# The last 128 tokens of an expert layer take the gathered path instead of the last 96, and are selected first

## The chip, the cores and the metric

The kernel runs on 1 core of one Trainium2 chip. The metric is the device time of the whole program in microseconds, lower is better.

## The reference

Two transformer layers over 512 tokens of width 1024, in float32. The first layer, the two attention mixers of the second and the norms are not touched by the change. The part that matters is the last step, `peer_ffn`: 16384 experts, each one row of `expert_u` and one of `expert_v`; every token has 8 heads, and every head picks 16 experts as sums of two sub-keys.

```python
def peer_ffn(x, w_q, sub_keys, expert_u, expert_v):
    q = _rms((xt @ w_q).reshape(T, P_HEADS, P_KEY_DIM))
    s1 = einsum('thd,hnd->thn', q[..., :half], sub_keys[:, 0])     # T x 8 x 128
    s2 = einsum('thd,hnd->thn', q[..., half:], sub_keys[:, 1])
    v1, i1 = top_k(s1, 16)
    v2, i2 = top_k(s2, 16)
    cand = (v1[..., :, None] + v2[..., None, :]).reshape(T, 8, 256)
    vals, ci = top_k(cand, 16)
    e = take(i1, ci // 16) * 128 + take(i2, ci % 16)               # T x 8 x 16
    g = softmax(vals)
    a = einsum('cd,ckd->ck', xc, expert_u[ec])
    w = gc * gelu(a)
    return einsum('ck,ckd->cd', w, expert_v[ec])
```

## The kernel before

**Layout.** The program runs both layers one after the other; the expert part takes the second half. Engines meet at counted semaphores, and each engine's program is written out by hand in the order in which it runs (`block.tensor` for PE, `block.scalar` for ACT, `block.vector` for DVE, `block.gpsimd` for POOL, `block.sync` for SP, which issues the loads and stores). The tokens lie on the columns of the moving operand, the features on the partitions, except in the selection, where a tile of 128 tokens lies on the partitions.

**Two paths for the experts.** For the first `TD` = 416 tokens (`T` - `RARE`) the kernel computes all 16384 experts: 128 *units* of 128 experts each. A unit of `u_in` is loaded into a ring of four slots (`u_load`), split into a high and a low part (`high` on ACT, line 1393; the low part on POOL in `column`, line 2162, for the first `U_PLAIN` = 52 units, and on DVE in `weight_low`, line 1978, for the others), and multiplied by the high and low parts of the normalised tokens (`u_unit`, 24 matmuls of 416 columns, line 1036). ACT takes the gelu (`gelu_unit`, line 1426), and SP stores it to `gelu` in HBM. The low parts alternate between two buffers, so the split of unit e waits for unit e - 2. The picked gates are put into a table of all experts by products of one-hot matrices: DVE makes those of 16 tokens (`one_hots`, lines 2007 to 2011), PE multiplies them (`spread`, line 1057, two banks of 4 tokens for each unit), ACT evacuates (line 1433), and SP stores a slab of 32 tokens, 2 MB, in two halves of a pair of blocks (`store`). There are `SLABS` = 13 slabs, done beside 4 units each. In the last stage (V) the table and the gelu are loaded again in quads of four units (`quad`), multiplied (`weigh`), split (`w_high`, `low`) and used as the moving operand against units of `v_in` (`v_unit`), 24 matmuls a unit again.

For the last `RARE` = 96 tokens the kernel gathers the picked rows instead. They lie on partitions in two blocks: 64 tokens, each on two partitions, and 32 tokens, each on four (`RARE_BLOCKS`), so that the 128 picks need 64 + 32 = 96 gathers of 128 rows of 4 KB (`rare_slot`). `u_gather` (POOL, line 2173) fetches into one of six slots, `dot` (DVE, line 1986) multiplies by the transposed token and sums; after the gelu and the gates, `v_gather` (line 2183) fetches the rows of `v` and `add_row` (DVE, line 2058) adds them up. At the end PE folds the partitions of a token together with small matmuls (lines 1075, 1076).

**Order.** PE: scores of the keys for four tiles of tokens (line 1011), transposes of the last 96 tokens (lines 1022 and 1028, evacuated by ACT to SBUF), 52 units without one-hots, transposes of the picks (line 1087), 52 units with two banks of one-hot products behind each, 24 units alone, then the 128 units of V. DVE: the selection of tiles 0 to 3 (lines 1906 to 1945) during the first 52 units, then the gates, one-hots, conversions and dots: 6 dots in 8 units in the loop, and the 58 left over spread over the last 23 units. Selection of a tile: the top 16 of 16 lists of 128 (`top16`), all 256 sums, the top 16 of 8 lists of 256, then for both index halves a comparison, a product and a sum over 2048 elements. ACT's Exp of all scores stands behind the gelu of unit 47.

Of the kernel before, what the change touches and what calls it, by code (L numbers as in the profile page):

```python
# [7 lines left out]
ALU = mybir.AluOpType  # L8
# [7 lines left out]
P = 128  # L16
# [34 lines left out]
RARE_BLOCKS = [(64, 2), (32, 4)]  # L51
RARE = sum(n for n, _ in RARE_BLOCKS)
TD = T - RARE
SLABS = TD // TB
RARE_AT = [0, PICKS // 2]
RARE_SLOTS = sum(PICKS // k for _, k in RARE_BLOCKS)
U_SLOTS, V_SLOTS = 6, 6
SPREAD_DOTS = 6
BANK_T = T // N_KEYS
U_PLAIN = 52  # L60
# [81 lines left out]
def rare_slot(s, i=0, per=0):  # L142

    m, r = divmod(s, 3)
    if r < 2:
        return 0, i * (per // 3 * 2) + (RARE_AT[0] + 2 * m + r)
    return 1, i * (per // 3) + (RARE_AT[1] + m)


# [13 lines left out]
def _ready(out):  # L163
# [10 lines left out]
    return "out_ready", base[kind] + j + 1  # L174

# [22 lines left out]
def build(nc, xT_in, par_in, pT_in, cst_in, stream, pos_in, u_in, v_in, rows_in, out, dense, gelu):  # L198
    with ExitStack() as ctx:
# [3 lines left out]
        def sem(name):  # L203
# [116 lines left out]
        cand = sb("cand", [P, E_H, E_K, E_K], c=ch)  # L320
        tv = sb("tv", [P, 2, E_H, E_K], c=ch)
        ti = sb("ti", [P, 2, E_H, E_K], mybir.dt.uint32, c=ch)
        tif = sb("tif", [P, 2, E_H, E_K], BF16, c=ch)
        cv = sb("cv", [P, E_H, E_K], c=ch)
        ci = sb("ci", [P, E_H, E_K], mybir.dt.uint32, c=ch)
        cm = sb("cm", [P, 2, E_H, E_K], mybir.dt.uint32, c=ch)
        cmf = sb("cmf", [P, 2, E_H, E_K], BF16, c=ch)
# [4 lines left out]
        oh = sb("oh", [P, E_H, E_K, E_K], BF16, c=ch)  # L332
        places = sb("places", [P, E_K], BF16, c=ch)
# [10 lines left out]
        wsp = sb("wsp", [P, 2, 2, T], F32R, c=ex)  # L344
        acc = sb("acc", [P, D], c=ex)
        rare = sb("rare", [P, U_SLOTS, D], c=ex)
        ex.close()
        rows_of = [rare[:, k, :] for k in range(U_SLOTS)]
        xts = [hnt[:, :, :].rearrange("p a t -> p (a t)"), xt2[:, :]]
        accs = [acc, acc2]  # L350
        dots, share, place = (rstd[:, k * RARE_SLOTS:(k + 1) * RARE_SLOTS] for k in range(3))
        place = place.bitcast(mybir.dt.uint32)
        folds = [rstd[:, 3 * RARE_SLOTS:3 * RARE_SLOTS + 64], rstd[:, 3 * RARE_SLOTS + 64:3 * RARE_SLOTS + 96]]
# [10 lines left out]
        tk_sub, tk_exp, sel_ready, selt_done = (sem(v) for v in ("tk_sub", "tk_exp", "sel_ready", "selt_done"))  # L364
# [68 lines left out]
        def _(sp_):  # L433
# [118 lines left out]
        def _(pe):  # L552
# [452 lines left out]
            for t in range(TT):  # L1005
# [55 lines left out]
            def v_unit(i, j, first=False, last=False):  # L1061
# [1300 lines left out]
```

## Time and profile before

| | |
|---|---|
| Three runs | 2704.39, 2709.26 and 2712.55 us, median 2709.26 us |
| The profiled execution | 2706.09 us, its span 2704.2 us |
| PE busy | 2585.8 us, 96% of the span |
| PE weight loads busy | 2228.3 us, 82% |
| DVE busy | 1788.3 us, 66% |
| ACT busy | 897.9 us, 33% |
| POOL busy | 1263.4 us, 47% |
| DMA | 491.88 MB, mean 182 GB/s |
| Mean granted clock of PE | 0.985 of full speed |

"Busy" is the time in which an engine runs at least one instruction; matmuls overlap one another in the records, so their mean duration is longer than the distance from one to the next. PEld is the loading of weights, which runs beside the matmuls. The DMA share is the mean busy share of the 16 DMA engines. Times in rows are microseconds from the start of the span.

### The profile page before, as it was taken

The numbers are of one execution on the slowest core, as the hardware profiler recorded it, in microseconds if no ns is written. First come the engines' busy times: TensorE is split into PE (matmuls) and PEld (weight loads), VectorE is DVE, ScalarE is ACT, GpSimd is POOL, SyncE is SP. The second block draws the span as 40 slices with busy tenths as digits, with TensorE's granted clock in tenths as the row PEclk, the third lists the DMA queues.
The fourth block names the chain that finished last, engine by engine and source line by source line (L and its number), as shares of the span: only waits on it lengthen the run. The fifth ranks groups of instructions, "written<-read, shape, count | busy, mean of one in ns | idle before, by whom it ended". The sixth has DMA issues, their size and how long they took to land.

```text
span 2704.2 us, 37346 instructions
## 1 busy us (share of the span) xinstructions
PE 2585.8 (96%) x13264; PEld 2228.3 (82%) x13264; DVE 1788.3 (66%) x2768; ACT 897.9 (33%) x1525; POOL 1263.4 (47%) x615
## 2 busy tenths in 40 slices
PE   6999999999998999998999999999999899999999
PEld 4777778888876777443878999999999899999999
DVE  7899983272234544766448996777778666676766
ACT  2323222101122224665224444344433233333332
POOL 5888888887875541000773555311147222222221
PEclk9999999999999998999999999999999999999999
DMA  4343334333322223000333555899999977887884
GB/s 146 130 138 128 134 122 140 128 107 125 122 100 91 86 86 129 1 1 1 120 116 102 158 159 153 266 301 302 301 343 418 364 296 293 309 303 294 297 300 165
DMA packets 176227, 491.88 MB, mean 182 GB/s; under 512 B 13840, under 2 KB 83600, under 8 KB 176144
## 3 DMA queue, kind: packets, MB, share of 16 engines
q1 hardware_dynamic: 148496, 390.15, 41.6%
q0 software_dynamic: 27648, 100.68, 10.4%
q8 instruction: 46, 0.75, 0.1%
q14 instruction: 37, 0.30, 0.0%
HBM read 434.14 MB, written 56.62 MB: 181 GB/s over the span
## 4 chain that ended last, share of the span: by engine, by line
PE 76%; DVE 7%; issue 7%; POOL 5%; DMA 3%; ACT 2%; SPq 0%; POOLq 0%; DVEq 0%; ACTq 0%
PE ps L1036 31%; PE ps L567 31%; POOL spl L2162 3%; PE ps L965 2%; PE ps L1057 2%; DMA rare<-rows_in,rstd 2%; PE ps L942 1%; PE ps L658 1%; POOL rare L2173 1%; PE ps L925 1%; PE ps L583 1%; DVE hnt L1521 1%; DVE hl L1525 1%; PE ps L921 1%; PE ps L830 1%
## 5 line engine op out<-in xcount | busy, mean ns | idle before, releaser
L567 PE MATMUL ps<-hh,spl 128*128 128x512 f32 x2064 | 654.4, 396 | 19.0 <-DVE hl L1525 7.2
L2095 POOL TENSOR_TENSOR spl<-ring,zero 128x1024 fp32r<-128x1024 f32 (+1 forms) x180 | 368.2, 2046 | 523.4 <-PE ps L567 457.2
L1036 PE MATMUL ps<-hh,spl 128*128 128x416 f32 x2048 | 574.0, 356 | 18.7 <-POOL spl L2162 7.5
L1036 PE MATMUL ps<-wsp,spl 128*128 128x416 f32 x3072 | 577.0, 349 | 4.1 <-DVE spl L1978 4.1
L1036 PEld LDWEIGHTS ps<-wsp,spl 128*128 128x128 f32 x3072 | 573.4, 188 | 5.4 <-DVE spl L1978 4.4
L1393 ACT ACTIVATE spl<-ring 128x1024 fp32r<-128x1024 f32 x256 | 271.3, 1060 | 719.7 <-PE ps L1036 707.3
L567 PEld LDWEIGHTS ps<-hh,spl 128*128 128x128 f32 x2064 | 391.0, 189 | 115.3 <-issue 15.5
L2097 POOL TENSOR_TENSOR spl<-ring,spl 128x1024 fp32r<-128x1024 f32 (+1 forms) x180 | 479.4, 2663 | 14.1
L1978 DVE TENSOR_TENSOR spl<-ring,spl 128x1024 fp32r<-128x1024 f32 x204 | 249.6, 1224 | 250.2 <-ACT spl L1393 250.0
L1036 PEld LDWEIGHTS ps<-hh,spl 128*128 128x128 f32 x2048 | 386.9, 189 | 28.7 <-issue 13.9
L567 PE MATMUL ps<-hl,spl 128*128 128x512 f32 x1032 | 404.9, 392 | 0.0
L1036 PE MATMUL ps<-hl,spl 128*128 128x416 f32 x1024 | 361.0, 353 | 0.0
L2183 POOL DMA_INDIRECT rare<-v_in,rstd x96 | 135.0, 1406 | 427.1 <-DVE acc L2058 404.7
L2173 POOL DMA_INDIRECT rare<-rows_in,rstd x96 | 134.7, 1403 | 270.0 <-DVE rare L1986 246.5
L567 PEld LDWEIGHTS ps<-hl,spl 128*128 128x128 f32 x1032 | 196.0, 190 | 40.5 <-issue 1.6
L2162 POOL TENSOR_TENSOR spl<-ring,spl 128x1024 fp32r<-128x1024 f32 x52 | 131.6, 2532 | 143.6 <-ACT spl L1393 143.6
L1036 PEld LDWEIGHTS ps<-hl,spl 128*128 128x128 f32 x1024 | 194.0, 189 | 1.3
L2058 DVE SCALAR_TENSOR_TENSOR acc<-rare,rstd,acc 128x1024 f32<-128x1024 f32 x96 | 122.8, 1279 | 4.6 <-DVE acc L2058 1.1
L567 PE MATMUL ps<-acth,spl 128*128 128x512 f32 x352 | 109.0, 390 | 2.5 <-DVEq L1702 1.7
L1340 ACT ACTIVATE pr<-ps,st,rr 128x31 f32<-128x31 f32 (+4 forms) x128 | 71.3, 557 | 64.1 <-DVE st L1850 62.2
L1986 DVE SCALAR_TENSOR_TENSOR rare<-rare,hnt 128x1024 f32<-128x1024 f32 x64 | 77.8, 1220 | 10.4 <-DMA rare<-rows_in,rstd 10.1
L1846 DVE TENSOR_REDUCE st<-ps 128x1 f32<-128x31 f32 (+4 forms) x128 | 52.9, 413 | 46.6 <-PE ps L929 37.8
(353 smaller groups left out, 3344.9 us busy)
## 6 DMA issues: line engine op xcount, KB each, us to landing
ring<-stream_in SPq DMA_DIRECT2D x196, 704.0 KB, 4.0
ring<-u_in SPq DMA_DIRECT2D x128, 512.0 KB, 3.9
ring<-v_in SPq DMA_DIRECT2D x128, 512.0 KB, 4.6
gelu<-gst SPq DMA_DIRECT2D x128, 208.0 KB, 4.1
dense<-stage SPq DMA_DIRECT2D x13, 2048.0 KB, 11.2
gl<-gelu SPq DMA_DIRECT2D x32, 832.0 KB, 5.1
gw<-dense SPq DMA_DIRECT2D x32, 832.0 KB, 6.9
x<-x_in SPq DMA_DIRECT2D x4, 512.0 KB, 6.0
```

What stands on the lines that cost most here:

```text
L567: m = pe.matmul(ps[:, bank, :], w[:, part, k0 + k * n:k0 + k * n + P], rhs(k), start=first and k == 0 and part == 0 and rhs is high, stop= ...
L1036: m = pe.matmul(ps[:, bank, 0:TD], w[:, part, k0 + k * P:k0 + (k + 1) * P], rhs(k), start=first and k == 0 and part == 0 and rhs is high, ...
L1340: eng.activation(pr[:, n % 2, qt, 0:nk], ps[:, qt, 0:nk], ACT.Exp, bias=st[:, n % 2, qt, 3:4], scale=root_of(n, qt), accum_out=st[:, n % 2 ...
L1393: eng.activation(spl[:, j % 2, 0, 0:D], ring[:, j % RING, 0:D], ACT.Copy).then_inc(hi_done, 1)
L1978: dve.tensor_tensor(spl[:, at % 2, 1, 0:D], ring[:, at % RING, 0:D], spl[:, at % 2, 0, 0:D].bitcast(F32), ALU.subtract).then_inc(lo_done, 1)
L1986: dve.scalar_tensor_tensor(out=rows_of[row], in0=rows_of[row], scalar=1.0, in1=xts[block], op0=ALU.mult, op1=ALU.mult, accum_out=dots[:, o ...
L2058: dve.scalar_tensor_tensor(out=accs[block][:, :], in0=rows_of[s % V_SLOTS], scalar=dots[:, one_at(at)], in1=accs[block][:, :], op0=ALU.mul ...
L2095: pool.tensor_tensor(w[:, 0, 0:n], ring[:, j, 0:n], zero[:, :].to_broadcast([P, n]), ALU.add).then_inc(wt_high, 1)
L2097: pool.tensor_tensor(w[:, 1, 0:n], ring[:, j, 0:n], w[:, 0, 0:n].bitcast(F32), ALU.subtract).then_inc(wt_low, 1)
L2162: pool.tensor_tensor(spl[:, j % 2, 1, 0:D], ring[:, j, 0:D], spl[:, j % 2, 0, 0:D].bitcast(F32), ALU.subtract).then_inc(lo_done, 1)
L2173: pool.indirect_dma_start(rows_of[s % U_SLOTS], None, rows_in, bass.IndirectOffsetOnAxis(place[:, at:at + 1], 0))\
L2183: pool.indirect_dma_start(rows_of[s % V_SLOTS], None, v_in.rearrange("b a d -> (b a) d"), bass.IndirectOffsetOnAxis(place[:, at:at + 1], 0 ...
```

## The change

`RARE` becomes 128: the whole last tile of tokens takes the gathered path, one token on each partition, so 128 gathers of rows of u and 128 of v, and no folding at the end. `TD` becomes 384, `SLABS` 12, and `U_PLAIN` 60; so the units are 60 plain, 48 with one-hots and 20 alone. The slots for rows become eight. The tile is selected first (`TILE_ORDER`), its expert numbers (`place`) are made right behind it, and POOL issues the first 44 gathers between its conversions of units 12 to 59 (`gathers_by`). 36 dots are done in the selection of the other three tiles, four at each of nine places; 8 in 8 units in the loop with one-hots; the other 44 over the last 19 units. The transposed tokens stay in PSUM (banks 6 and 7), so the one-hot products alternate between two banks instead of four.

The selection is rebuilt: of the 256 sums only 112 are made (`N_CAND`: all 16 of the first 4 rows, 4 of each other row), and the index is found by a subtraction in float32 and a minimum over the bits read as unsigned integers, instead of comparison, product and sum in bf16. Some of its operands move to PSUM (`right`, `best`, `key_at`, `bound`).

```diff
-RARE_BLOCKS = [(64, 2), (32, 4)]
-RARE = sum(n for n, _ in RARE_BLOCKS)
+RARE_TILE = TT - 1
+RARE = P
-U_SLOTS, V_SLOTS = 6, 6
-SPREAD_DOTS = 6
+ROW_SLOTS = 8
+EARLY_DOTS, SPREAD_DOTS = 36, 8
+TILE_ORDER = [RARE_TILE] + list(range(RARE_TILE))
+FRONT, BACK = 4, 4
+N_CAND = FRONT * E_K + (E_K - FRONT) * BACK
+SPREAD_BANKS = 2
+PLACED, FIRST_DOTS = 12, 24
-U_PLAIN = 52
+U_PLAIN = 60
+def gathers_by(e):
+    if e < FIRST_DOTS:
+        return min(2 * (e - PLACED + 1), ROW_SLOTS)
+    return ROW_SLOTS + EARLY_DOTS * (e - FIRST_DOTS) // (U_PLAIN - FIRST_DOTS)
...
 @block.tensor
             for c in range(DC):
-                bank = ps[:, 4 + c // 4, c % 4 * P:(c % 4 + 1) * P]
-                for half in range(2):
-                    for rows in (hh, hl):
-                        m = pe.matmul(bank[half * 64:(half + 1) * 64, :], rows[:, c, T - 64:T].bitcast(F32), cc("ident"),
-                                      start=rows is hh, stop=rows is hl)
...
                 for rows in (hh, hl):
+                    m = pe.matmul(xt[:, c * P:(c + 1) * P], rows[:, c, TD:T].bitcast(F32), cc("ident"),
+                                  start=rows is hh, stop=rows is hl)
...
-            with pe.Fori(0, U_PLAIN // 4) as i:
+            with pe.Fori(0, U_PLAIN // 4 - 1) as i:
                 for j in range(4):
                     u_unit(i, j)
+            for j in range(3):
+                u_unit(U_PLAIN // 4 - 1, j)
             pe.wait_ge(sel_ready, 1)
+            for k in range(2):
+                turn_picks(k, 4 + k)
+            u_unit(U_PLAIN // 4 - 1, 3)
+            pe.wait_ge(picks_read, 1)
+            turn_picks(2, 4)
...
 @block.vector
+            def some_dots(k):
+                for s in range(k * EARLY_DOTS // (3 * RARE_TILE), (k + 1) * EARLY_DOTS // (3 * RARE_TILE)):
+                    dot(s)
...
+            for n, i in enumerate(TILE_ORDER):
+                dve.wait_ge(sk_evac, n * 8 + 8)
                 top16(...)                                 # first level, as before
+                if n == 1:
+                    dve.wait_ge(xt_done, 1)
+                if n:
+                    some_dots(3 * n - 3)
+                step(dve.tensor_copy(right, tv[:, 1, :, :]))
+                for a0, a1, bn, at in ((0, FRONT, E_K, 0), (FRONT, E_K, BACK, FRONT * E_K)):
+                    ...                                    # cand: 64 and 48 sums a head
+                for k in range(2):
+                    o = dve.tensor_tensor(key_at[:, k, :, :], ti[:, k, :, :], steps..., ALU.add)
+                top16([(cv[:, h, :], ci[:, h, :], cand[:, h, :]) for h in range(E_H)])
+                if n:
+                    some_dots(3 * n - 2)
+                ...                                        # ce, then eight small operations on the index
                 for k in range(2):
-                    step(dve.tensor_tensor(oh, cmf..., places..., ALU.is_equal))
-                    step(dve.tensor_tensor(oh, oh, tif..., ALU.mult))
-                    step(dve.tensor_reduce(sel..., oh, AX_X, ALU.add))
+                    step(dve.tensor_tensor(far, key_at..., place_at..., ALU.subtract))
+                    step(dve.tensor_reduce(sel..., far.bitcast(uint32), AX_X, ALU.min))
+                if n:
+                    some_dots(3 * n - 1)
+                else:
+                    dve.scalar_tensor_tensor(out=place, ...).then_inc(place_ready, 1)
...
 @block.gpsimd
-            with pool.Fori(0, U_PLAIN // RING) as i:
+            with pool.Fori(0, PLACED // RING) as i:
                 for j in range(RING):
                     column(i, j)
-            for s in range(RARE_SLOTS):
+            s = 0
+            for e in range(PLACED, U_PLAIN):
+                column(e // RING, e % RING)
+                while s < gathers_by(e):
+                    u_gather(s)
+                    s += 1
+            for s in range(s, PICKS):
                 u_gather(s)
```

## Rows read from the trace of the kernel before

**Rows 1.** By windows: length, busy PE, PEld, DVE, ACT, POOL; PE clock, DMA share, GB/s.

```profile
1453.00:1699.00 246.00, 238.47 (x1251) 232.32 (x1248) 214.79 (x721) 112.22 (x133) 126.98 (x50) 1.00 0.51 151
1709.00:1991.00 282.00, 282.00 (x2038) 271.57 (x2039) 220.63 (x232) 123.01 (x202) 50.41 (x41) 0.99 0.92 300
1991.00:2121.00 130.00, 115.19 (x596) 111.01 (x594) 98.33 (x142) 38.86 (x55) 86.31 (x58) 0.97 1.02 405
2121.00:2690.00 569.00, 568.60 (x3038) 567.61 (x3039) 389.28 (x410) 189.06 (x252) 126.81 (x90) 1.00 0.78 289
```

**Rows 2.** Timeline of PE at line 830; start us, us, engine, line.

```profile
995.51 0.42 PE L830 MATMUL ps<-spl,hh 128*128 128x280 f32 x2
...
997.85 0.42 PE L830 MATMUL ps<-spl,hh 128*128 128x280 f32 x2
```

**Rows 3.** The chain that ended last; start us, us, what.

```profile
1384.77 11.01 PE ps L567 x48
...
1699.38 1.32 PE ps L1087 x12
1701.62 4.56 DMA rare<-rows_in,rstd
...
2121.40 566.32 PE ps L1036 x3024
```

**Rows 4.** Timeline of PE before unit 0.

```profile
1428.54 16.17 PE L1011 MATMUL ps<-ring,qp 128*128 128x128 f32 x128
1445.73 0.45 PE L1022 MATMUL ps<-cst,hh 128*64 128x128 f32 x4 [1.02 <-ACT s_sb L1409]
```

**Rows 5.** Timeline of POOL in the plain stage.

```profile
1498.90 2.39 POOL L2162 TENSOR_TENSOR spl<-ring,spl 128x1024 fp32r<-128x1024 f32 x1 [3.41 <-ACT spl L1393]
...
1517.85 2.38 POOL L2162 TENSOR_TENSOR spl<-ring,spl 128x1024 fp32r<-128x1024 f32 x1 [3.41 <-ACT spl L1393]
```

**Rows 6.** Timeline of DVE, one tile of the selection.

```profile
1547.03 3.20 DVE L1916 MAX8 tv<-s_sb 128x8 f32<-128x128 f32 x16
...
1566.42 2.49 DVE L1928 TENSOR_TENSOR cand<-tv 128x2048 f32<-128x2048 f32 x1
1568.95 2.72 DVE L1916 MAX8 cv<-cand 128x8 f32<-128x256 f32 x8
...
1584.31 1.55 DVE L1932 TENSOR_TENSOR ce<-cv 128x128 f32<-128x128 f32 x1
...
1586.10 0.23 DVE L1935 TENSOR_SCALAR cm<-ci 128x128 uint32<-128x128 uint32 x1
...
1598.23 3.31 DVE L1942 TENSOR_TENSOR oh<-oh,tif 128x2048 bf16<-128x2048 bf16 x1
```

**Rows 7.** Costliest groups, the gathers of expert_u.

```profile
L2173 POOL DMA_INDIRECT rare<-rows_in,rstd x96 | 134.7, 1403 | 270.0 <-DVE rare L1986 246.5
```

**Rows 8.** Timeline of POOL, a gather right behind another.

```profile
1708.84 1.97 POOL L2173 DMA_INDIRECT rare<-rows_in,rstd  x1 [0.30 <-issue]
```

**Rows 9.** Timeline of DVE in the spread stage.

```profile
1855.16 1.22 DVE L1978 TENSOR_TENSOR spl<-ring,spl 128x1024 fp32r<-128x1024 f32 x1 [1.81 <-ACT spl L1393]
...
1860.85 1.22 DVE L1978 TENSOR_TENSOR spl<-ring,spl 128x1024 fp32r<-128x1024 f32 x1
1861.98 1.22 DVE L1986 SCALAR_TENSOR_TENSOR rare<-rare,hnt 128x1024 f32<-128x1024 f32 x1
...
1866.19 1.23 DVE L1978 TENSOR_TENSOR spl<-ring,spl 128x1024 fp32r<-128x1024 f32 x1 [2.98 <-ACT spl L1393]
```

**Rows 10.** DMA queues from 1740 to 1980; packets, MB, share of 16 engines.

```profile
q1 hardware_dynamic: 56704, 54.90, 70.6%
q0 software_dynamic: 4743, 17.27, 21.4%
```

**Rows 11.** Timeline of ACT in V.

```profile
2401.16 1.06 ACT L1393 ACTIVATE spl<-ring 128x1024 fp32r<-128x1024 f32 x1 [2.98 <-PE ps L1036]
```

**Rows 12.** Timeline of DVE in V.

```profile
2408.59 0.59 DVE L2050 TENSOR_TENSOR wsp<-gl,wsp 128x416 fp32r<-128x416 f32 x1
```

More of the change, by code:

```diff
@@ L331, in build @@
         seven.close()
[L332 to L333 removed]
+        part4 = sb("part4", [P, E_H, E_K], mybir.dt.uint32, c=ch)
+        four = sb("four", [P, E_H, E_K], c=ch)
+        place_at = sb("place_at", [P, 2, E_H, E_K], c=ch)
+        far = sb("far", [P, E_H, E_K, E_K], c=ch)
+        steps = sb("steps", [P, E_K], c=ch)
         sel = sb("sel", [P, TT, 3, E_H * E_K], c=ch)
@@ L1004, in _ @@
             n = 0
-            for t in range(TT):
+            for t in TILE_ORDER:
                 for b in range(4):
@@ L1093, in _ @@
                     spread(i, 2 * k + 1)
-            for k in range(4):
-                u_unit(U_PLAIN // 4 + SLABS - 1, k)
-                spread(SLABS // 2, 2 * k)
-                spread(SLABS // 2, 2 * k + 1)
             with pe.Fori(U_PLAIN // 4 + SLABS, N_KEYS // 4) as i:
@@ L1403, in _ @@
             n = 0
-            for t in range(TT):
+            for t in TILE_ORDER:
                 for b in range(4):
@@ L1414, in _ @@
             eng.sem_inc(gelu_done, 4)
-            eng.wait_ge(xt_done, 1)
-            for k in range(2):
-                eng.activation(hnt[:, k, :], ps[:, 4 + k, :], ACT.Copy).then_inc(xt_ready, 1)
-            for k in range(2):
-                eng.activation(xt2[:, k * T:(k + 1) * T], ps[:, 6 + k, :], ACT.Copy).then_inc(xt_ready, 1)
             def gelu_unit(i, j):
@@ L1920, in top16, with dot @@
                     step(o)
+            def dot(s, i=None):
+                row = s % ROW_SLOTS
+                count = 16 * (s // ROW_SLOTS + 1)
+                dve.wait_ge(u_row[row], count if i is None else i * 16 + count)
+                at = s if i is None else i * SPREAD_DOTS + s
+                dve.scalar_tensor_tensor(out=rows_of[row], in0=rows_of[row], scalar=1.0, in1=xt, op0=ALU.mult, op1=ALU.mult,
+                                         accum_out=dots[:, one_at(at)]).then_inc(dot_done, 1)
@@ new lines, in _ @@
+                dve.tensor_scalar(part16, ci[:, :, :], 4, None, ALU.logical_shift_right)
+                step(dve.tensor_scalar(part4[:, :, :], ci[:, :, :], 2, None, ALU.logical_shift_right))
+                step(dve.scalar_tensor_tensor(out=right, in0=part4[:, :, :], scalar=float(FRONT - FRONT * E_K // BACK),
+                                              in1=part16, op0=ALU.add, op1=ALU.max))
+                dve.tensor_scalar(place_at[:, 0, :, :], right, float(N_KEYS), None, ALU.mult)
+                step(dve.tensor_scalar(four[:, :, :], right, float(BACK), float(FRONT * (E_K - BACK)), ALU.mult, ALU.add))
@@ L2019, in _ @@
                     for s in range(j * SPREAD_DOTS // 4, (j + 1) * SPREAD_DOTS // 4):
-                        dot(s, b)
+                        dot(EARLY_DOTS + s, b)
                     weight_low(U_PLAIN + 2 * j + 2, b, 8)
-            s, last = SLABS // 2 * SPREAD_DOTS, U_PLAIN + 4 * SLABS
-            for j in range(2):
-                at = SLABS // 2 * 4 * GB + j * GB
-                one_hots(j, SLABS // 2, slice(at, at + GB))
-                weight_low(last - 4 + 2 * j + 1)
-                dot(s)
-                s += 1
-                weight_low(last - 4 + 2 * j + 2)
-            first, left = last + 1, RARE_SLOTS - s
+            s, last = EARLY_DOTS + SLABS // 2 * SPREAD_DOTS, U_PLAIN + 4 * SLABS
+            first, left = last + 1, PICKS - s
             for e in range(first, N_KEYS):
@@ L2067, in unit_pair @@
                     weigh(*to_weigh)
-                for s in range(p * 12 // 8, (p + 1) * 12 // 8):
+                for s in range(2 * p, 2 * p + 2):
                     add_row(i, s)
```

215 lines of the change are left out of this document (84 added, 131 removed).

## The prediction

> **What bounds the kernel now.** I cut the dense part into four stages with the busy times by window [rows 1], then asked for each stage what its slowest resource is. *Plain* (1453 to 1699): 52 units of expert rows; PE 97% busy, DVE 87% on the selection. *Spread* (1709 to 1991): units with the one-hot products between them; PE 100%, DMA share 0.92. *Tail* (1991 to 2121): 24 units while DVE works off the dots; PE only 89%, DMA share 1.02. *V* (2121 to 2690): PE 100%, DVE 68%, DMA 0.78. So PE sets the end everywhere but in the tail, where DMA does. PE's price in V: 3038 matmuls in 568.6 us, 187 ns each, so the 24 of a unit take 4.49; in U 188 ns and 4.52.
>
> What does PE's time hang on, columns or weight loads? The loads are busy 567.61 of V's 569 us, which looks like a limit. But in PE's timeline at line 830, from 995.51 to 997.85, 18 matmuls of 280 columns, each with a 128x128 load, take 2.34 us: 130 ns each [rows 2]. And the chain of work shows 48 matmuls of 512 columns in 11.01 us: 229 ns [rows 3]. 130, 188, 229 for 280, 416, 512 columns is a line of about 0.42 ns a column plus 13. A load overlaps the matmul before it and does not set the pace at 416. 384 columns give 175 ns: **0.32 us less for each unit**, 4.20 in U and 4.17 in V.
>
> **The change part by part.**
>
> *Start.* The transposes of x took from 1445.7 to 1453.0, PE idle on nothing else [rows 4]. Now 16 products of two instructions with full 128-column loads; the 128 of that kind in front of them took 126 ns each, so 4.0 us. Unit 0 starts at 1449.8. The four ACT copies of x go.
>
> *Plain stage, 60 units instead of 52.* Four units last 18.95 us (POOL's conversion from 1498.90 to 1517.85 [rows 5]): four times 4.52 plus 0.85 of stall, since once in four units ACT loads tables twice, and unit done, table, high part, low part (2.4 us on POOL) is longer than a unit. That chain doesn't shrink, so the stall grows by the 0.32 that the unit loses: 4 x 4.20 + 1.17 = 17.97. Before: 12 x 18.95 + 4 x 4.52 = 245.5 (246.2 by the trace). After: 14 x 17.97 + 4 x 4.20 + 0.7 = 269.1, to 1718.9; with nine transposes (12 took 1.3 [rows 3]) 1719.9.
>
> *What is put on DVE there.* A tile of the selection takes 57 us [rows 6]: first top-16 19.4 (1547.03 to 1566.42), sums 2.5, second top-16 15.4 (to 1584.31), then small ones 2.6 and six one-hot passes 17 (the last but one starts at 1598.23, the last is 2.3 long, which is also what a pass takes that POOL doesn't lengthen). New: 19.4; sums of 112 places for 256, 1.1; the top-16 on 112: 8 maxima on 256 take 2.72, 16 on 128 take 3.20, so 0.34 and 0.20 each and about 0.18 on 112, and by that the 15.4 become 9; some 13 small operations at 0.23: 3; four passes at 2.3 instead of six: 9.3. Together 42, four tiles 168. The 36 dots cost 1.22 each [rows 9], 44: 212 us from 1435.7, to 1648 if nothing waits. But dots wait for gathers, and gathers come by unit number. Unit e's conversion on POOL starts at about 1451 + 4.5(e - 1). Gather s from 8 on is issued at e = s + 17, and the first, issued at 1701.62, landed some 6 us later [rows 3]. Gather 35 goes out at 1683 and lands by 1689, so the last dot ends near 1698; Exp on ACT stands behind the gelu of unit 55 (1703), so the gates are ready at about 1707. PE asks for them after unit 58, at 1714. Slack 7 us; nothing on the path.
>
> *What is put on POOL there.* One gather a unit: 1.40 on average [rows 7], 1.97 where one follows on another, and 0.30 between two [rows 8]. 2.4 + 1.7 = 4.1 fits into a unit's 4.49; at 2.27 each it is 4.67 and costs 35 x 0.18 = 6. Here each stands alone, nearer the average, and I take 0. What is queued behind a gather is the next conversion, and PE behind that; gather s waits for dot s - 8. The tightest is dot 24 (done about 1662, wanted about 1667).
>
> *Into the spread.* Unit 60, then PE waits for the first one-hots, as before (unit end 1705 to 1709.0); now the gates come one unit later but the index copies lie earlier: wait 2.5. First spread at 1726.7.
>
> *Spread, 48 units instead of 52.* The period is 5.51 (DVE's conversions at 1855.16 and 1866.19 are two units apart [rows 9]); now 5.19. 47 x 5.19 + 0.94 = 244.9, to 1971.6. Two banks instead of four: ACT is busy 44% [rows 1] and evacuates right behind its unit, with a whole unit before PE wants the bank, so 0; if ACT came late it would cost what it is late. DVE: between two conversions lie 5.69 us, so one-hots 4.55 and a conversion 1.14; with another conversion and two dots at 1.14 9.1 in 10.4. DMA is the tight one. The queue view [rows 10] gives 21.4% to gathers and 70.6% to the rest. Gathers go up by 8/6 x 44.05/41.5 = 1.415, to 30%; the rest by 1.03 to 73%: 1.03 to 1.04, against 1.02 in the tail, where it is full [rows 1]. So DMA and PE meet. From 0 (slots hide it) to 20 us; I take 5: 1976.6.
>
> *Tail, 20 units instead of 24.* Before, 405 GB/s x 130 us = 52.7 MB. After: 4 loads of 0.52 less, saves 1.2 less, tables 0.4 less, and 36 gathers still to issue instead of 52 (44 dots less 8 in slots; 58 less 6): 12.1 less, 40.6 MB, at 405 100 us. PE alone, with the last 5 us of gelu, product and conversion before the first V unit (now at 2121.4 [rows 3]), gives 89. I take 98: V begins at 2074.6.
>
> By the Trainium skill (DMA: Bandwidth & Descriptors, Where 436 GB/s comes from) about 358 GB/s binds between HBM and SBUF; the window of the tail [rows 1] shows 405, so the trace doesn't agree, and by that rule the tail would be 113.
>
> *V.* One row more for four units: DVE +0.32 a unit, in all 3.4 of 4.17. The tightest path is a pair with two rows: unit done (ACT starts at 2401.16 [rows 11]) to the end of the second low part (2409.18 [rows 12]) is 8.0, against 2 x 4.17 = 8.35. It fits by 0.3, and every pair is now such. DMA per unit 1.44 MB instead of 1.34, in 4.17: 345 GB/s, share 0.92. So 128 x 0.32 = 41.0 off the 582.8 from 2121.4 to 2704.2: 541.8. End 2616.4.
>
> The profiled execution's own time is 1.9 over its span, so 2618; the median shown is 3 above that time: **2619**.
>
> **The rivals.**
>
> *Transfers pile up in spread and tail.* For it: 1.03 to 1.04 asked of 1.02, and the stores of 2 MB between the loads. Against it: slots are asked for four unit pairs ahead. Two stores per 8 units at 2 us each, 24 more: about 2643. 0.14.
>
> *POOL and DVE hold up the plain stage.* Gathers at 2.27 (+6), or a selection that is not shorter than 57 a tile (the change not doing what it says): the last dots near 1711, eight us late for POOL. +8 to +15: 2632. 0.09.
>
> *Weight loads bind.* For it: the loads' 99.8% of V. Against: the 280 columns [rows 2]. Then no unit shrinks, 107 units and V lose 0.32 each: +75, 2694. 0.04. The Trainium skill (Perfetto Trace Analysis, Identifying the Most-Contended Engine) takes the busy share of weight loads for the measure of how near TensorE is to its roofline, and by that rule V can't shrink; line 830 speaks against it.
>
> *DMA can't give more than it gives in these stages* (the other side). If 300 GB/s of spread and 299 of V were ceilings and not demands, V would need 1.442/0.299 = 4.82 a unit (+42 against now) and the spread 47.0 for 8 units (282): 1726.7 + 282 + 100 + 625 = 2734, time 2736. V turns slower from a ceiling below 1.442/4.495 = 321. Against: 405 over 130 us. 0.05.
>
> **How the numbers follow.** Forecast 0.66, piled transfers 0.14, plain stage 0.09, loads 0.04, ceiling 0.05, something unseen 0.02 (counted slower with the last). The forecast's own range: 2604 (spread 0, tail 89) to 2632. The range for 8 in 10 takes in the first two rivals: 2600 to 2655. A measurement of this kernel tells 0.3% (8 us) from no change. Faster 0.92, same 0.02, slower 0.06.
>
> **What would show it.** PE at 175 ns a matmul, V at 4.17 a unit; POOL's conversions 4.5 apart in the plain stage with gathers between them; gates before unit 59; DMA above 1.0 in the spread with a period of 5.2; tail 95 to 100 for 20 units; V at 345 GB/s. Wrong: a V period above 4.25, a wait for weights on ACT (ring loads late) in the spread, or PE waiting on POOL's conversion more than once in four units.

## The result and the profile after

The changed kernel takes 2621.76 us, the median of 4 runs (2617.54 to 2626.19), beside 2710.7 us for the kernel before (4 runs, 2704.39 to 2712.55). The ratio is 0.9678, with a 95% interval from 0.9657 to 0.9699: 3.2% faster. The prediction said 2619. The profiled execution took 2623.1 with a span of 2621.3. Of the timed runs below, one of e11 (7162 us) and one of the kernel before beside e0 to e3 (8138 us) lie far off all others and are left out of medians and ratios.

These are its four stages by windows, cut where the new stages lie. The columns are those of [rows 1], which they answer.

```profile
core 0: us, PE busy (x) PEld busy (x) DVE busy (x) ACT busy (x) POOL busy (x), PEclk, DMA share, GB/s
1449.00:1719.00 270.00, 256.23 (x1463) 250.78 (x1463) 211.33 (x859) 125.73 (x149) 181.60 (x102) 1.00 0.75 243
1727.00:1968.00 241.00, 239.18 (x1841) 231.78 (x1842) 215.89 (x236) 111.79 (x184) 44.45 (x47) 0.99 0.97 330
1968.00:2078.00 110.00, 97.40 (x555) 96.32 (x555) 84.30 (x121) 34.68 (x51) 49.48 (x48) 0.94 1.03 405
2078.00:2610.00 532.00, 530.22 (x3030) 523.55 (x3030) 417.37 (x438) 185.54 (x252) 157.33 (x119) 1.00 0.90 332
```

The order of limits is the old one: PE everywhere, DMA in the tail. A part of the gathered path's transfers has moved into the plain stage (243 GB/s after 151), and the tail, four units shorter, takes about 100 us instead of 130. DVE is busier in V, 417 of 532 us after 389 of 569.

The chain of waits through the end of the tail and through V answers to the last row of [rows 3]:

```profile
2046.62 14.74 DMA rare<-rows_in,rstd
2061.38 1.23 DVE rare L1912 x2
...
2069.90 16.53 DMA gelu<-gst
2086.58 4.37 DMA ring<-v_in
2090.97 1.07 ACT spl L1386
2093.81 512.67 PE ps L1025 x2928
```

The last dot waits for its row, a saved block of activations takes 16.5 us to leave, V's fifth weight unit is loaded only after it, and then PE runs 2928 matmuls in one piece, 175.1 ns each on average, where it took 187.3 before. Most of them start 173 ns after the one in front; what the average has above that comes up in e8.

For comparing executions I cut each by four marks that every kernel has: the first transpose of x, the start of the first matmul of the first spread, that of the last spread's last matmul, and V's first unit (the end of V's first low part). That takes out the untouched 1440 us ahead, which differ by up to 11 us from one execution to the next (first transpose at 1441.3 to 1452.4). The marks come from rows such as these, of the changed kernel, by line with the first and last start:

```profile
L1017 PE MATMUL ps<-cst,hh x16: 275/275/348, 1448.8 to 1452.1; 128*128 128x128 f32 x16
L1046 PE MATMUL ps<-oh x768: 218/218/238, 1728.8 to 1974.0; 128*128 128x128 f16 x192
2071.76 0.55 DVE L2037 TENSOR_TENSOR wsp<-gl,wsp 128x384 fp32r<-128x384 f32 x1
```

The lengths in us, with the median of the timed runs:

| kernel | to the first spread | spread | tail | V to the end | median |
|---|---|---|---|---|---|
| before | 263.3 | 283.3 | 129.0 | 582.9 | 2710.7 |
| changed | 280.0 | 245.2 | 98.3 | 549.0 | 2621.8 |
| the changed kernel again (e0) | 280.0 | 245.3 | 100.8 | 547.8 | 2621.6 |
| 416 columns (e1) | 295.3 | 259.9 | 95.1 | 590.4 | 2690.3 |
| no early dots (e2) | 279.9 | 245.3 | 151.4 | 546.1 | 2671.2 |
| key passes twice (e3) | 292.6 | 243.7 | 98.1 | 551.9 | 2633.0 |
| 45 early dots (e4) | 280.1 | 245.0 | 88.3 | 547.0 | 2605.9 |
| 54 early dots (e5) | 280.1 | 245.2 | 87.5 | 545.7 | 2605.3 |
| stores in halves (e6) | 279.9 | 245.0 | 102.1 | 548.0 | 2620.7 |
| V start lighter (e7) | 280.1 | 243.6 | 96.2 | 547.2 | 2622.3 |
| adds apart (e8) | 280.0 | 245.2 | 100.7 | 544.2 | 2617.2 |
| adds apart, 45 dots (e9) | 279.9 | 245.2 | 89.0 | 540.6 | 2602.5 |
| e9, loads ahead of the wait (e10) | 279.9 | 245.0 | 92.0 | 540.5 | 2601.0 |
| 416 columns, rows 2048 bytes apart (e11) | 295.2 | 261.3 | 96.3 | 587.3 | 2685.9 |

The first column repeats within 0.2 us where no edit touches it, the spread within 2, the tail within 3; the medians of the changed kernel in two sets of runs agree to 0.2. Rows that no edit meant to touch also show how far single executions scatter: V's first unit, from its first matmul to the second unit's, takes 5.75 to 7.0 us in the traces of the changed kernel, e0, e2, e4, e7, e8 and e9.

### The profile page after: what moved, and what is told of

Read it like the earlier page. It is cut to its first block, busy times and chain, and to the rows that moved or that the text cites. A ratio compares the mean times of both kernels' runs of the same rounds, so it can differ in the third digit from the quotient of the medians.

```text
span 2621.3 us, 37105 instructions
## 1 busy us (share of the span) xinstructions
PE 2494.9 (95%) x13021; PEld 2137.6 (82%) x13021; DVE 1783.5 (68%) x2863; ACT 891.5 (34%) x1517; POOL 1299.4 (50%) x687
## 4 chain that ended last, share of the span: by engine, by line
PE 79%; DVE 8%; issue 4%; POOL 3%; DMA 3%; ACT 2%; ACTq 0%; SPq 0%; DVEq 0%; POOLq 0%
PE ps L1025 33%; PE ps L564 32%; PE ps L962 2%; POOL spl L2147 2%; PE ps L1046 2%; PE ps L655 1%; PE ps L939 1%; PE ps L922 1%; DVE rare L1912 1%; PE ps L580 1%; DMA ring<-u_in 1%; DVE hnt L1505 1%; DVE hl L1509 1%; ACT spl L1386 1%; PE ps L918 1%
## 5 line engine op out<-in xcount | busy, mean ns | idle before, releaser
L1025 PE MATMUL ps<-hh,spl 128*128 128x384 f32 x2048 | 540.6, 339 | 22.3 <-POOL spl L2147 13.8
L1025 PE MATMUL ps<-wsp,spl 128*128 128x384 f32 x3072 | 542.2, 337 | 5.9 <-DVE spl L1980 4.1
L1025 PEld LDWEIGHTS ps<-wsp,spl 128*128 128x128 f32 x3072 | 533.3, 189 | 12.8 <-DVE wsp L2037 5.2
L564 PEld LDWEIGHTS ps<-hh,spl 128*128 128x128 f32 x2064 | 389.8, 189 | 115.4 <-issue 15.4
L1025 PEld LDWEIGHTS ps<-hh,spl 128*128 128x128 f32 x2048 | 373.5, 189 | 28.5 <-ACT gst L1414 23.6
L2166 POOL DMA_INDIRECT rare<-v_in,rstd x128 | 167.7, 1310 | 366.6 <-DVE hnt L2044 344.6
L1025 PE MATMUL ps<-hl,spl 128*128 128x384 f32 x1024 | 344.0, 336 | 0.0
L1980 DVE TENSOR_TENSOR spl<-ring,spl 128x1024 fp32r<-128x1024 f32 x196 | 239.2, 1220 | 146.4 <-ACT spl L1386 133.7
L2147 POOL TENSOR_TENSOR spl<-ring,spl 128x1024 fp32r<-128x1024 f32 x60 | 143.9, 2398 | 103.4 <-ACT spl L1386 103.0
L1912 DVE SCALAR_TENSOR_TENSOR rare<-rare,ps 128x1024 f32<-128x1024 f32 x128 | 150.6, 1215 | 46.3 <-DMA rare<-rows_in,rstd 46.0
L2044 DVE SCALAR_TENSOR_TENSOR hnt<-rare,rstd,hnt 128x1024 f32<-128x1024 f32 x128 | 166.1, 1298 | 12.2 <-DVE hnt L2044 11.3
L1830 DVE TENSOR_REDUCE st<-ps 128x1 f32<-128x31 f32 (+4 forms) x128 | 52.9, 414 | 46.7 <-PE ps L926 38.0
```

Of the source, the lines that this page charges most:

```text
L564: m = pe.matmul(ps[:, bank, :], w[:, part, k0 + k * n:k0 + k * n + P], rhs(k), start=first and k == 0 and part == 0 and rhs is high, stop= ...
L1025: m = pe.matmul(ps[:, bank, 0:TD], w[:, part, k0 + k * P:k0 + (k + 1) * P], rhs(k), start=first and k == 0 and part == 0 and rhs is high, ...
L1912: dve.scalar_tensor_tensor(out=rows_of[row], in0=rows_of[row], scalar=1.0, in1=xt, op0=ALU.mult, op1=ALU.mult, accum_out=dots[:, one_at(at ...
L1980: dve.tensor_tensor(spl[:, at % 2, 1, 0:D], ring[:, at % RING, 0:D], spl[:, at % 2, 0, 0:D].bitcast(F32), ALU.subtract).then_inc(lo_done, 1)
L2044: dve.scalar_tensor_tensor(out=acc, in0=rows_of[s % ROW_SLOTS], scalar=dots[:, one_at(i * 16 + s)], in1=acc, op0=ALU.mult, op1=ALU.add).th ...
L2147: pool.tensor_tensor(spl[:, j % 2, 1, 0:D], ring[:, j, 0:D], spl[:, j % 2, 0, 0:D].bitcast(F32), ALU.subtract).then_inc(lo_done, 1)
```

## The experiments

**The changed kernel again (e0).**

> The changed kernel itself, run beside the other three on one chip, so that they can be set against it: 2618 to 2626 us.

2621.57 us (2618.32 to 2625.78), ratio 0.967 [0.9651, 0.9688]. It is what e1 to e3, of the same chip, are set against. e4 to e11 ran on two other chips, where the kernel before took 2710.3 and 2709.8 us beside 2711.2 here, so differences to the changed kernel across chips are uncertain by some 2 us.

**Columns alone undone (e1).**

```
- ps[:, bank, 0:TD] ... hh[:, k, 0:TD] ... wsp[:, j % 2, 0, 0:TD]
+ ps[:, bank, 0:WIDE] ... hh[:, k, 0:WIDE] ... wsp[:, j % 2, 0, 0:WIDE]      # WIDE = 416
+ dve.tensor_copy(wsp[:, :, :, TD:WIDE], <zeros>)                            # once, ahead of V
```

> The changed kernel with one part undone: every matmul of the dense units takes 416 columns instead of 384 (U's from tokens 384 to 415 too, whose results nobody reads; V's from 32 columns of zeros). Transfers, gathers, dots and added rows stay as they are. Mine, that columns set PE's pace: 187 ns a matmul instead of 175; plain +15 (four units 18.95 again), spread +15 (48 x 0.32), tail 0 to +6 (it waits for DMA), V +41: in all +65 to +77 over the changed kernel, about 2693. Rival, that weight loads set the pace: 0 to +5, the period stays 175. If V's period at 384 columns were held by DVE or DMA already, V would give back less than 41.

2690.26 us, ratio 0.9924 [0.9906, 0.9941]: 68.7 over the changed kernel, inside the 65 to 77. The table gives +15.3 to the first spread, +14.7 in the spread, -3.2 in the tail and +41.4 in V (against the changed kernel's first profile). So 69 of the 89 us that the change brings are gone when each matmul takes 32 columns more again. Weight loads don't set the pace. The chain of waits of e1 has V's 122 gapless units:

```profile
2118.51 553.34 PE ps L1026 x2928
```

553.34 is 4.54 a unit. I had expected 4.49 or the old 4.48: one part of V got slower that columns don't explain. So V's 41 us are a mixture: some 41 for the columns, about 5 less because a lateness of the changed kernel (e8) is gone at 416 columns, and about 7 more, 128 times 0.05, that stay open.

**The same with the old distance between rows (e11).** One guess at that part: the rows of the split weights lie 1664 bytes apart in e1 and lay 2048 apart before.

> The kernel with 416 columns, with the four rows of V's split weights 2048 bytes apart as before the change instead of 1664. Its V units were 4.53 us apart, before the change 4.48, with nothing waiting. If the distance of the rows does it: V's units at 4.48 and -6 us against the kernel with 416 columns. If something else in V does (two adds a pair, more gathers): no change.

2685.93 us (three runs, 2683.4 to 2688.69), ratio 0.9914 [0.9891, 0.9937], against the -6 that the distance alone would have brought from e1's 2690.26. V's high parts come 4.520 apart instead of 4.533, before the change 4.480. So by the trace the distance is about a quarter of it, and the 0.04 a unit that are left stay open: no engine waits in them by the profile. The medians differ by 4, across two chips, and their intervals overlap.

**Early dots back into the tail (e2).**

```
- EARLY_DOTS, SPREAD_DOTS = 36, 8
+ EARLY_DOTS, SPREAD_DOTS = 0, 8
```

> The changed kernel with no dots among the selection: the 36 early ones go to the tail, which then has 80 dots and 36 gathers more. Mine, that the tail is set by DMA's volume: 36 x 0.524 MB = 18.9 MB more at 405 GB/s: +47 us (and the plain stage the same length), about 2669. Rival, that the tail has room and the early dots only fill DVE: 0 to +10. DVE bound instead: 36 dots x 1.22 = 44 on top of 84 busy would be 128, under the 157 of DMA.

2671.22 us, ratio 0.985 [0.9832, 0.9867]: +49.7, by volume 47. The tail grows from 98 to 101 us to 151.4, the other stages stay. By windows, e2's tail:

```profile
1972.00:2123.00 151.00, 102.45 (x484) 97.21 (x480) 116.53 (x179) 31.68 (x47) 82.13 (x79) 0.85 1.03 410
```

DMA is full at 410 GB/s and DVE has room (116.5 of 151). The tail is set by volume over what DMA moves. Had the 36 early dots stayed in the tail, the change would have been worth about 40 us and not 89.

**The selection as long as before (e3).**

```
- for k in range(2):        # the two passes that read out a key: differences, then the least
+ for k in (0, 1, 0, 1):
```

> The changed kernel with the four passes that read out the keys done twice in each tile (same result): +9.3 us a tile, so that the three later tiles take about what a tile took before the change. Mine, that the selection hides behind PE: tile 0 ends at 1495 instead of 1486 and unit 12's gathers wait till then only (its conversion is at 1507), later tiles use the 43 us that DVE spends waiting for gathers: 0 to +4. Rival, that the shorter selection is what makes the plain stage fit: each late dot holds a gather on POOL, the conversion behind it and PE: +15 to +28.

2632.99 us, ratio 0.9707 [0.969, 0.9725]: +11.4. Mine (0 to +4) was wrong, and the rival too high. The path to the first spread is 12.6 longer. The chain of waits of e3 lies on DVE from 1584.65 on and ends so:

```profile
1578.02 6.61 DMA rare<-rows_in,rstd
1584.65 1.23 DVE rare L1912 x2
...
1713.34 2.30 DVE far L1957
...
1717.99 1.24 DVE rare L1912 x2
1720.47 2.37 POOL spl L2147
1722.88 5.95 PE ps L1025 x24
```

A gather stands on POOL behind dot s - 8, the conversion behind the gather, PE behind the conversion. By the waits of e3 PE stood 8.4 us at one time for the conversion, where in the changed kernel the longest such wait is 1.0:

```profile
PE ps L1025 <- POOL spl L2147: 23.2, 18, 8.4
POOL rare L2157 <- DVE rare L1912: 13.7, 5, 9.6
```

My mistake was to take DVE's waits for gathers, 42.9 us in the changed kernel, as one sum of room. They all lie in front of 1586, the longest before the second tile's last dots (timeline of DVE, the changed kernel):

```profile
1571.51 1.22 DVE L1912 SCALAR_TENSOR_TENSOR rare<-rare,ps 128x1024 f32<-128x1024 f32 x1 [19.98 <-DMA rare<-rows_in,rstd]
...
1585.72 1.22 DVE L1912 SCALAR_TENSOR_TENSOR rare<-rare,ps 128x1024 f32<-128x1024 f32 x1 [3.78 <-DMA rare<-rows_in,rstd]
```

In e3 the two tiles selected first take 2 x 9.3 = 18.6 us of it (the waits fall by 19.0, to 23.9). The other two, behind 1586, add 18.6 with nothing to hide in but the 7 us that the prediction had as slack: 11.6, for 12.6 measured. POOL's wait of 9.6 for a dot, in front of a gather and the conversion behind it, is where that reaches PE.

**More early dots (e4, e5).**

```
- EARLY_DOTS, SPREAD_DOTS = 36, 8          - PLACED, FIRST_DOTS = 12, 24
+ EARLY_DOTS, SPREAD_DOTS = 45, 8          + PLACED, FIRST_DOTS = 12, 15         # e4
+ EARLY_DOTS, SPREAD_DOTS = 54, 8          + PLACED, FIRST_DOTS = 8, 12          # e5
```

> The changed kernel with 45 dots instead of 36 among the selection, their gathers one a unit from unit 15 instead of 24 on; the tail keeps 35 dots and 27 gathers of 0.52 MB. Mine, that volume sets the tail while PE waits 12.6 us in it: 4.7 MB less at 405 GB/s, -8 to -11 (PE's floor takes the rest), about 2612. Rival, from the doubled passes (+28 us of DVE cost +11): 9 dots are 11 us more on DVE in the plain stage and would be paid there: -11 + 5 or worse, -6 to 0.

> As the kernel with 45, with 54 dots among the selection, gathers from unit 8 on, 54 over the 48 units from unit 12. Volume alone: -9.4 MB, but PE has only the 12.6 us of its waits to give in the tail: -10 to -13. DVE gets 22 us more in the plain stage, near the 28 that cost 11: I expect -3 to -8 in all, less than with 45. If the plain stage has room after all: -12.

e4: 2605.91 us, ratio 0.9621 [0.96, 0.9642], 15.7 below the changed kernel and more than the 8 to 11 that I had expected. e5: 2605.33, ratio 0.9614 [0.9593, 0.9635], 16.2 below, where I had expected 3 to 8, or 12 if the plain stage had room. The plain stage costs nothing more in either, 280.1 to the first spread. The two tiles selected last do get more to do, 6 dots in e4 and 12 in e5 (14.6 us at 1.22 each, not much less than e3's 18.6). But the ninth gather and those behind it start from unit 15 and 12 instead of 24, so the rows come earlier: DVE waits 21.0 and 16.9 us for them where the changed kernel waits 42.9, and the wait of 20 us is gone. That is 22 and 26 us less of waiting for 11 and 22 us more of dots. By the timelines of DVE the selection's last dot ends 254.7 us after the first transpose in the changed kernel, 244.9 in e4 and 250.1 in e5, but 274.8 in e3, where the work came without earlier rows. The tail ends at 88.3 and 87.5, near the 89 that I had given for PE alone, and there e5 gains nothing more. By windows, the tail of the changed kernel, of e4 and of e5:

```profile
1974.00:2072.00 98.00, 85.81 (x484) 84.86 (x481) 75.25 (x109) 31.65 (x47) 43.42 (x42) 0.96 1.03 405
```

```profile
1967.00:2054.00 87.00, 83.20 (x479) 82.44 (x477) 65.81 (x92) 31.28 (x46) 33.25 (x34) 1.00 1.04 411
```

```profile
1978.00:2065.00 87.00, 83.18 (x480) 82.86 (x479) 56.18 (x75) 31.38 (x47) 24.36 (x25) 1.00 0.98 361
```

The DMA share is above 1 in the first two, 0.98 at 361 GB/s in the third. The tail gives 10 to 12 of e4's 15.7 us and V one or two; the rest is not located (a median is uncertain by about 2, and chips differ by 1.4).

**The store ahead of a load (e6).** In the tail ACT waits 11.2 us for a weight unit. The timeline of SP's queue in the changed kernel shows the last 2 MB store issued in front of it:

```profile
1977.12 0.57 SPq L490 DMA_DIRECT2D dense<-stage  x1
1981.10 11.80 SPq L468 DMA_DIRECT2D ring<-u_in  x1
```

e6 issues each store as two of half the size, two loads apart.

```
- if j == 1: store(i, k)
+ if j in (1, 3): store(i, k, j // 2)       # half the rows of dense each
```

> The changed kernel with every store of a finished 2 MB block of gates issued as two of 1 MB, two weight loads apart. One theory: in the tail ACT waits 11.2 us for a weight load that SP issued 11.8 us late behind the last whole store; a shorter store lets the load in between: -4 to -8. Rival, volume sets the tail and only the order changes: -1 to +1. A store that ends a unit pair later could also hold up ACT's next evacuation: + some us in the spread.

2620.73 us, ratio 0.9675 [0.9654, 0.9697]: nothing. The edit didn't bring the loads forward either: in the timeline of SP's queue in e6 the load behind the last half store, issued at 1982.09, took 18.5 us to issue. ACT's longest wait for a load is 12.4 instead of 11.2. The result agrees with the rival, that volume sets the tail; that no other order would help isn't shown by this one.

**Less asked of DMA at the start of V (e7).**

```
  v_load(0, j) ...
- if j < 3: quad(0, j)
+ if j < 2: quad(0, j)                      # the third after v_load(1, 1)
+ if s >= 2: pool.wait_ge(acc_done, 2)      # V gathers 2 to 7, beside the wait for the last dot
```

> The changed kernel with less asked of DMA where V starts: the third quad of activations and gates (1.6 MB) is loaded after V's sixth weight unit instead of its third, and gathers 2 to 7 of V's rows (3.1 MB) wait until the first row is added. Mine: ACT's 5.6 us wait for a V weight unit at 2091, which PE repeats, goes: -5 to -6 and V lasts 542 to 543 as in the prediction. Rival, that the stores and loads ahead of V hold it up, or that the delayed transfers are missed two units later: 0.

2622.27 us, ratio 0.9681 [0.9659, 0.9704]: nothing, against the -5 to -6 that I had expected. My reading of the start of V was wrong. ACT's 5.6 us wait at 2091 costs PE only 1.9, because two converted units lie ahead of it: the fourth unit's last matmul starts at 2091.69 and the fifth's first at 2093.81, 2.1 later, where 0.17 is the usual distance. In e7 ACT no longer waits for that load, but PE still stops there, for 1.2 instead of 2.1, so the edit could win about 1 us. More is lost where I hadn't looked. By windows, around V's first unit and around the first unit of the tail that comes after a long wait:

```profile
1996.00:2006.00 10.00, 3.23 (x19) 2.91 (x17) 1.23 (x2) 1.96 (x3) 0.94 (x1) 0.86 1.04 414
2006.00:2012.00 6.00, 5.87 (x23) 5.88 (x24) 6.00 (x10) 0.91 (x2) 3.39 (x4) 0.66 0.97 347
2012.00:2018.00 6.00, 6.00 (x36) 6.00 (x36) 4.57 (x8) 2.76 (x4) 3.29 (x4) 1.00 0.99 343
...
2072.00:2079.00 7.00, 6.58 (x22) 6.62 (x23) 5.29 (x6) 0.00 (x0) 3.84 (x4) 0.55 1.02 421
2079.00:2086.00 7.00, 7.00 (x43) 7.00 (x42) 2.72 (x3) 2.94 (x4) 0.00 (x0) 1.00 1.04 417
```

After a wait PE's granted clock is 0.66 and 0.55, near the lower of its two levels (1.2 GHz), and back at 1.00 (2.4 GHz) in the next stretch. From its first matmul to the next unit's, the unit at 2006 takes 6.1 us and V's first 7.0, for 4.2. So these two waits cost their length and 2 to 3 us more. V's first unit took 6.1 before the change too, for 4.5, so more than half of that was in my sum already.

**V's added rows apart (e8).**

```
- for k in (2 * p, 2 * p + 1): weight_low(k); low(k)
- weigh(...);  add_row(2 * p);  add_row(2 * p + 1)
+ for k in (2 * p, 2 * p + 1): weight_low(k); low(k); [weigh(...) if k is odd]; add_row(k)
```

> The changed kernel with V's two added rows of a unit pair taken apart: one after each unit's low parts instead of both after the second's. Mine: V's units come 4.16 and 4.20 to 4.26 us apart by turns because the path over DVE (low parts, product, two adds with 0.20 between them, low parts) is longer than two units; apart it has over a us of slack in every unit: -3 to -5, units 4.16 apart throughout. Rival: the longer turns come from the gathers' and loads' DMA or from PE itself: 0.

2617.15 us (2613.53 to 2621.19), ratio 0.9661 [0.9645, 0.9677]: 4.4 below the changed kernel, as expected; the intervals overlap, and the chips differ by 1.4, but the trace is plain: V's units come 4.160 apart on average for 4.202, which is 5.4 us in 128 units. ACT's high parts of V's weights, which follow the end of a unit, in the changed kernel and then in e8:

```profile
2300.31 1.07 ACT L1386 ACTIVATE spl<-ring 128x1024 fp32r<-128x1024 f32 x1 [2.81 <-PE ps L1025]
2304.47 1.06 ACT L1386 ACTIVATE spl<-ring 128x1024 fp32r<-128x1024 f32 x1 [2.69 <-PE ps L1025]
2308.69 1.06 ACT L1386 ACTIVATE spl<-ring 128x1024 fp32r<-128x1024 f32 x1 [2.74 <-PE ps L1025]
2312.85 1.06 ACT L1386 ACTIVATE spl<-ring 128x1024 fp32r<-128x1024 f32 x1 [2.69 <-PE ps L1025]
2317.11 1.06 ACT L1386 ACTIVATE spl<-ring 128x1024 fp32r<-128x1024 f32 x1 [2.79 <-PE ps L1025]
```

```profile
2301.55 1.06 ACT L1386 ACTIVATE spl<-ring 128x1024 fp32r<-128x1024 f32 x1 [2.69 <-PE ps L1025]
2305.71 1.06 ACT L1386 ACTIVATE spl<-ring 128x1024 fp32r<-128x1024 f32 x1 [2.69 <-PE ps L1025]
2309.87 1.06 ACT L1386 ACTIVATE spl<-ring 128x1024 fp32r<-128x1024 f32 x1 [2.69 <-PE ps L1025]
2314.03 1.06 ACT L1386 ACTIVATE spl<-ring 128x1024 fp32r<-128x1024 f32 x1 [2.69 <-PE ps L1025]
```

4.16, 4.22, 4.16, 4.26 by turns in the first, 4.16 throughout in the second. The waits of the changed kernel from 2100 to 2600 have the reason, and those of e8 have no such line:

```profile
PEld ps L1025 <- DVE wsp L2037: 3.1, 17, 0.2
```

Every second unit of the changed kernel stands behind the low part that DVE makes of the weights.

**Both (e9), and SP's order (e10).** e10 moves the wait for the last saved activations behind the next four weight loads.

```
- for j in range(4): sp_.wait_ge(gelu_saved[j], ...)
  for j in range(RING): v_load(1, j)
+ for j in range(4): sp_.wait_ge(gelu_saved[j], ...)
```

> Both: 45 dots among the selection and V's adds apart. If the one takes time from the tail and the other from V's period, they add: -16 and -4, about 2602. If the kernel with 45 dots had V's period at 4.16 already: 2606.

> As e9, and SP issues V's weight loads 4 to 7 before it waits for the last saved activations instead of behind that wait. In the changed kernel ACT's wait at 2091 stood behind a save that took 16.5 us and then that load. Mine: with 45 dots PE hardly waits there any more, so 0 to -2 against e9. If the wait is still there in most executions: -5.

e9: 2602.53 us, ratio 0.9608 [0.9594, 0.9622]; V takes 540.6, the tail 89.0. e10: 2600.97, ratio 0.96 [0.9586, 0.9615]; between the two nothing is told apart. Both beat the changed kernel by 19 to 21 us with intervals that don't touch its own.

## Why the prediction was right, point by point

The mechanism was right: columns set PE's pace, and volume sets the tail. How close the number came is in part luck. The sum ended at a span of 2616.4, the trace at 2621.3. The terms of that difference are +2.6 at the start, -0.5 to the first spread, -4.7 in the spread, +0.3 in the tail and +7.2 in V: a pile-up of transfers that didn't come cancels most of a lateness in V that I hadn't seen.

*Slips in the working.* 2618 and 3 are 2621, and the prediction's last step wrote 2619. The 3 was the distance of one profiled execution from the median, too: here the median lies 1.3 below the profiled execution. In the rival of a ceiling, 299 GB/s is what a unit's megabytes give at the old period; [rows 1] has 289 for V. The first gather's row in [rows 3] lands 4.6 us after 1701.62, not 6. None of these changes what the argument says, but with the right addition the forecast would have been 2621.

*PE's price.* A line of 0.42 ns a column plus 13 gave 175 ns at 384 columns. Right: 175.1 in V, 4.16 us for a unit that waits for nothing. e1 shows that it is columns. The Trainium skill (Perfetto Trace Analysis, Identifying the Most-Contended Engine) takes the busy share of weight loads, beside the share of peak arithmetic, for how near TensorE is to its limit, and the loads' 98% of V would read as one; the trace doesn't agree, since the loads were busy 99.8% before [rows 1] and V still became 6% shorter; their busy time for each matmul fell with it, from 186.8 to 172.8 ns.

*Start.* The transposes took from 1448.8 to 1452.3, 3.5 us for 4.0. They began 3.1 later than those of before, as all in front of them did: an execution's own scatter.

*Plain stage.* Four units 17.97 predicted; 17.9 by the trace. A tile of the selection took 46.7 us for 42. What was missed: two key sums of 128 elements in 2.23 and one shift in 2.18 while its neighbour took 0.28, all from the timeline of DVE:

```profile
1459.91 2.23 DVE L1937 TENSOR_TENSOR ps<-ti,steps 128x128 f32<-128x128 uint32 x2
...
1471.94 0.28 DVE L1946 TENSOR_SCALAR ps<-ci 128x128 uint32<-128x128 uint32 x1
1472.14 2.18 DVE L1947 TENSOR_SCALAR part<-ci 128x128 uint32<-128x128 uint32 x1
1474.35 0.30 DVE L1948 SCALAR_TENSOR_TENSOR ps<-part,ps 128x128 f32<-128x128 uint32 x1
```

A conversion ran on POOL from 1471.84 to 1474.24, and the shift, the first of them to write SBUF, ended with it; that POOL held it is argued from this, not tried. The miss cost little, if anything: to the first spread it took 0.5 less than forecast. e3 prices twice as much: 9.3 more a tile cost 11.4 in all. The rival of POOL and DVE put 2632 to a selection that is not shorter; it didn't happen, and e3, which makes it so, took 2633.

*Gathers on POOL.* 1.40 each from [rows 7] was too high. In the timeline of POOL they take 0.94 to 1.13, two between conversions too:

```profile
1503.51 2.40 POOL L2147 TENSOR_TENSOR spl<-ring,spl 128x1024 fp32r<-128x1024 f32 x1 [3.02 <-ACT spl L1386]
1506.08 1.13 POOL L2157 DMA_INDIRECT rare<-rows_in,rstd  x1 [0.17 <-issue]
1507.52 0.94 POOL L2157 DMA_INDIRECT rare<-rows_in,rstd  x1 [0.30 <-issue]
1508.48 2.39 POOL L2147 TENSOR_TENSOR spl<-ring,spl 128x1024 fp32r<-128x1024 f32 x1
```

*Gates.* DVE went on behind ACT's Exp at 1708.2, and PE asked for the gates at 1717: slack there, as the 7 us said. PE then waited 2.4 for the first one-hots (2.5).

*Spread.* The period is 5.16 for 5.19, the first unit takes 1.8 more than the others, as it did before (1.6), and the 5 us that I put down for DMA didn't come: its share was 0.97 where I had counted 1.03. The transfers didn't pile up there, and the rival falls, and so does that of a ceiling at 300 GB/s.

*Tail.* 98 for 20 units; 98.3 and 100.8 by the two traces. The Trainium skill (DMA: Bandwidth & Descriptors, Where 436 GB/s comes from) has about 358 GB/s, one core's half of its HBM, as what binds between HBM and SBUF; by that the tail would be 113, an estimate. This one core moved 405 to 411, so the trace doesn't agree.

*V.* This is the term that was mis-sized: 541.8 for a measured 549.0 (547.8 in e0). "It fits by 0.3, and every pair is now such" failed. The path over DVE itself is as long as it was, 7.98 us from ACT's start at 2304.47 to the end of the second low part, for 8.02 in [rows 11] and [rows 12]. These are its last steps by the timeline of DVE in V:

```profile
2308.04 1.28 DVE L2044 SCALAR_TENSOR_TENSOR hnt<-rare,rstd,hnt 128x1024 f32<-128x1024 f32 x1
2309.53 1.32 DVE L2044 SCALAR_TENSOR_TENSOR hnt<-rare,rstd,hnt 128x1024 f32<-128x1024 f32 x1 [0.20 <-DVE hnt L2044]
2310.77 1.21 DVE L1980 TENSOR_TENSOR spl<-ring,spl 128x1024 fp32r<-128x1024 f32 x1
2311.91 0.54 DVE L2037 TENSOR_TENSOR wsp<-gl,wsp 128x384 fp32r<-128x384 f32 x1
```

The 0.3 of room was counted between the wrong marks. ACT starts only 0.34 after the next unit's first matmul has begun (2304.13 here). And PE doesn't want the low part for a unit's first matmul but for its weight load, which goes 0.17 earlier, beside the last matmul of the unit in front. Together that is 0.5, more than the room. In the pair shown the load would have gone at 2312.34; it started at 2312.51, right behind the low part's end at 2312.45, and the unit's second matmul came 0.10 late. The one accumulator adds to it: before, two rows went into two accumulators in 2.71, now both go into one, the second waits 0.20 for the first, and the two take 2.81. On average a pair is late by 0.08, 5.4 us in 128 units. e8 gives that back by taking a row out of the path; how much one accumulator alone does isn't tried.

The rest lies at V's ends: 1.9 in front of the fifth unit (1.7 in e0) and about 1 in the first, which ran at the lower clock (nothing in e0, 5.8 us), less about 1 at the end, where nothing is folded any more. With the pairs' lateness and the stop at the fifth unit gone (e9), V takes 540.6, though its first unit still takes 6.5. V moved 332 GB/s for the 345 that I had counted.

## What to carry to other kernels

Read each stage's limit before you sum: here 32 columns fewer were worth 69 us where PE sets the time, and 19 MB of gathers moved from a stage where DMA is full to one where it isn't 50; if the two add, which no run tries, the wider gathered part costs the some 30 that they are above 89. Eight slots for rows instead of six, two banks instead of four and the order of the tiles were not undone one by one. Where a path "fits by 0.3", count from the marks at which the engine itself starts and wants it (here 0.5 in all), and go through the edits on it once more (here one accumulator for two). And an engine's waits are not one sum of room: 22 us more of dots were free where their rows also came earlier and the waits shrank by 26 (e5); 18.6 us of work behind the last wait were paid but for 7 (e3).

## What the runs showed of the hardware that I had not expected

- A gather's issue on POOL took 0.98 us on average in the changed kernel (128 of them) and 1.40 in the one before (96, [rows 7]); those of V's rows 1.31 and 1.41. Which of the differences around it does that isn't shown.
- After two waits in the changed kernel TensorE's granted clock lay at 0.66 and 0.55 over the next unit, which then took 6.1 and 7.0 us for 4.2. In e2, whose tail has the most waits, it was 0.85 over 151 us; in e4, with few, 1.00.
- The issue of a 0.5 MB load behind a 2 MB store held SP's queue for 11.8 us while DMA was full; with the store in halves one such issue took 18.5 us, and the kernel's time was the same.
- At 416 columns V's units took 4.53 us (4.52 with the rows 2048 bytes apart), where the kernel before needed 4.48 for the same columns. No wait shows, and this stays open.
- In V each weight load starts right after the matmul in front of its own. Where a unit's first load waited 0.16 us for DVE (2312.34 to 2312.51), its first matmul still started on time and its second came 0.10 late.
